# Identity products in eleven more waits, and one weight quarter of the second expert stage loaded early

## What is computed

```python
for layer in range(DEPTH_2):
    u = x * (1.0 + sc1) + sh1
    mix = _mixer(u, ...)
    x = _layernorm(DEEPNORM_ALPHA * x + (1.0 + g1) * mix, ...)
    u = x * (1.0 + sc2) + sh2
    ff = _dense_swiglu(u, ...) if layer % 2 == 0 else _moe_swiglu(u, ...)
    x = _layernorm(DEEPNORM_ALPHA * x + (1.0 + g2) * ff, ...)
```

## Time and profile before

| | us |
|---|---|
| median of 3 runs | 2059.11 |
| lowest and highest | 2055.4 and 2060.55 |
| profiled execution, its own time | 2051.38 |
| its span, first to last instruction | 2049.6 |
| TensorE busy in the span | 1951.5 (95%) |
| VectorE busy | 649.2 (32%) |
| ScalarE busy | 170.3 (8%) |
| mean granted clock of TensorE | 0.986 |

### The profile page before, as it was taken

How to read it: one execution, slowest core, us unless ns; L and a number is a source line. 1 busy time by engine, 2 the same in 40 slices (tenths; PEclk the granted TensorE clock), 3 DMA queues, 4 the chain that set the end, 5 groups by cost and what they waited for, 6 DMA issues and landing times.

```text
span 2049.6 us, 68398 instructions
## 1 busy us (share of the span) xinstructions
PE 1951.5 (95%) x31337; PEld 1567.6 (76%) x31337; DVE 649.2 (32%) x1411; ACT 170.3 (8%) x369; POOL 17.3 (1%) x66
## 2 busy tenths in 40 slices
PE   6999999999999989999999999998999999999996
PEld 4787468777777857648776577588999989989895
DVE  5586333222222232164332523530011110111104
ACT  2002010000000002000000110010000000000000
POOL 1000000000000000000000000000000000000000
PEclk9999999999999999999999999999999999999998
DMA  9998559999999995327766733279999999999992
GB/s 350 314 389 330 214 215 397 420 422 423 421 421 425 420 398 213 142 77 276 261 213 233 267 109 123 103 289 392 411 389 413 405 406 415 403 413 406 405 364 114
DMA packets 179139, 656.00 MB, mean 320 GB/s; under 512 B 16212, under 2 KB 20724, under 8 KB 170868
## 3 DMA queue, kind: packets, MB, share of 16 engines
q1 hardware_dynamic: 170528, 647.41, 80.5%
q0 software_dynamic: 1456, 5.24, 0.7%
q10 hardware_dynamic: 7076, 2.20, 0.5%
HBM read 653.76 MB, written 1.05 MB: 319 GB/s over the span
## 4 chain that ended last, share of the span: by engine, by line
PE 90%; DVE 5%; DMA 3%; issue 2%; SPq 0%; DVEq 0%; ACT 0%
PE ps L1844 88%; DMA ring<-in_moe_w_gate_dram 2%; PE ps L1852 1%; DMA ring<-in_w_ada_dram 1%; DVE stat L1103 0%; DVE arena L1508 0%; DVE arena L1303 0%; DVE hT L991 0%; DVE x L1212 0%; DVE tok L978 0%; DVE tok L1211 0%; DVE newton L971 0%; DVE hT L1086 0%; DVE x L1097 0%; DVE arena L1177 0%
## 5 line engine op out<-in xcount | busy, mean ns | idle before, releaser
L1844 PE MATMUL ps<-arena,ring 128*64 128x80 f32 (+2 forms) x25216 | 877.5, 230 | 23.2 <-issue 18.1
L1844 PEld LDWEIGHTS ps<-arena,ring 128*64 128x64 f32 (+1 forms) x25216 | 859.8, 138 | 50.3 <-issue 40.4
L1844 PE MATMUL ps<-hT,ring 128*128 128x256 f32 (+1 forms) x1680 | 359.4, 385 | 4.2 <-DVE stat L995 2.2
L1844 PEld LDWEIGHTS ps<-hT,ring 128*128 128x128 f32 (+1 forms) x1680 | 308.2, 189 | 51.0 <-issue 2.5
L1844 PE MATMUL ps<-ring,arena 128*64 128x512 f32 (+1 forms) x880 | 273.8, 595 | 1.5 <-DVE stat L1774 1.1
L1844 PE MATMUL ps<-arena 128*128 128x128 f32 (+6 forms) x1576 | 209.1, 307 | 14.0 <-DVE arena L1711 5.6
L1844 PEld LDWEIGHTS ps<-ring,arena 128*64 128x64 f32 (+1 forms) x880 | 104.5, 159 | 150.8 <-issue 147.2
L1844 PEld LDWEIGHTS ps<-arena 128*128 128x128 f32 (+4 forms) x1576 | 138.3, 166 | 67.6 <-issue 31.1
L1469 DVE MEMSET ps<- 128x480 f32 x68 | 28.9, 425 | 278.5 <-ACT arena L742 273.6
L1844 PE MATMUL ps<-ring,hT 128*128 128x512 f32 (+2 forms) x256 | 87.6, 500 | 0.0
L1844 PEld LDWEIGHTS ps<-ring,hT 128*128 128x128 f32 x256 | 46.1, 190 | 38.1 <-issue 36.2
(11 more groups left out here) (325 smaller groups left out, 797.9 us busy)
## 6 DMA issues: line engine op xcount, KB each, us to landing
ring<-in_moe_w_gate_dram SPq DMA_DIRECT2D x128, 704.0 KB, 8.0
ring<-in_moe_w_up_dram SPq DMA_DIRECT2D x128, 704.0 KB, 9.2
ring<-in_moe_w_down_dram SPq DMA_DIRECT2D x176, 512.0 KB, 10.5
ring<-in_w_gate_dram SPq DMA_DIRECT2D x32, 2048.0 KB, 14.8
ring<-in_w_up_dram SPq DMA_DIRECT2D x32, 2048.0 KB, 14.1
ring<-in_w_down_dram SPq DMA_DIRECT2D x32, 2048.0 KB, 12.3
ring<-in_w_in_dram SPq DMA_DIRECT2D x19, 2048.0 KB, 13.9
ring<-in_w_ada_dram SPq DMA_DIRECT2D x12, 2048.0 KB, 15.7
```

The source lines that it names most:

```text
L1844: ins = pe.matmul(*args, **kw)
```

## The change

Three things change. (1) `keep_busy` is called in eight more places of the run and with 5 instead of 3 in the three tile transposes: 21 identity products more. (2) SP loads the second gate quarter of expert 0's first half right behind the first eleven down pieces, after a wait for `x_normed` 7 (VectorE's first normed tile at the end of layer 1's mixer): three pieces go to free columns of another buffer and one to ring columns behind the held pieces. The gate's first quarter of the next half then takes the places where the second quarter was loaded before, at the same waits for `piece_used`. (3) TensorE does the first half of expert 0 in straight code, `first_half_in`, instead of a loop of two passes, because its second gate quarter is read from other places. That is 704 instructions of matmuls and weight loads more. Counts that the gate's semaphores are compared with become one quarter lower (`row_count`).

The diff, without blank context and without its part in `second_all`, which is not run:

```diff
@@ -271,6 +271,7 @@
         gate_row = [sem(f"gate_row{k}") for k in range(KQ)]
         up_row = [sem(f"up_row{k}") for k in range(KQ)]
         down_row = [sem(f"down_row{f}") for f in range(TH)]
+        early_row = [sem(f"early_row{k}") for k in range(KQ)]
         piece_used = sem("piece_used")
         gate_clear, y_clear = sem("gate_clear"), sem("y_clear")
         rows_ready = sem("rows_ready")
@@ -326,6 +327,8 @@
         held_gate = flat[:, GATE_AT:UP_AT].rearrange("p (k n) -> p k n", k=KQ)
         held_up = flat[:, UP_AT:DOWN_AT].rearrange("p (k n) -> p k n", k=KQ)
         held_down = flat[:, DOWN_AT:DOWN_AT + TH * D].rearrange("p (f n) -> p f n", f=TH)
+        EARLY_AT = DOWN_AT + TH * D
+        early_gate = [view(9600 + j * FH, FH) for j in range(KQ - 1)] + [flat[:, EARLY_AT:EARLY_AT + FH]]
         START = None
@@ -468,9 +471,12 @@
             def load_quarter(w, e, v, q, at, place, full, n):
                 for j in range(KQ):
                     if n is None:
                         left_by_ring(at + (j + 1) * FH)
+                    elif isinstance(n, int) and n == 1 and q == 0 and at == GATE_AT:
+                        sp.wait_ge(piece_used, j + 1)
                     else:
                         use = j + (at // QUARTER) * KQ
                         sp.wait_ge(piece_used, used_by(n, use) if q else used_by(n - 1, 2 * KQ + use))
@@ -491,12 +497,17 @@
             load_quarters(0, 0, 0, None)
             load_downs(0, 0, None)
-            for place, full, w, first in ((held_gate, gate_row, wg, 0), (held_up, up_row, wu, KQ)):
-                for j in range(KQ):
-                    sp.wait_ge(piece_used, first + j + 1)
-                    sp.dma_start(place[:, j, :], expert_cols(w, 0, 0, FH)[:, KQ + j, :]).then_inc(full[j], 16)
-            for q in range(2):
-                load_quarters(0, 1, q, 1)
+            sp.wait_ge(H["x_normed"], 7)
+            for j in range(KQ):
+                if j == KQ - 1:
+                    left_by_ring(EARLY_AT + FH)
+                sp.dma_start(early_gate[j], expert_cols(wg, 0, 0, FH)[:, KQ + j, :]).then_inc(early_row[j], 16)
+            load_quarter(wg, 0, 1, 0, GATE_AT, held_gate, gate_row, 1)
+            for j in range(KQ):
+                sp.wait_ge(piece_used, KQ + j + 1)
+                sp.dma_start(held_up[:, j, :], expert_cols(wu, 0, 0, FH)[:, KQ + j, :]).then_inc(up_row[j], 16)
+            load_quarter(wu, 0, 1, 0, UP_AT, held_up, up_row, 1)
+            load_quarters(0, 1, 1, 1)
             with sp.Fori(1, NE2) as e:
                 load_quarters(e, 0, 0, e * 2)
                 load_downs(e - 1, 1, e * 2)
@@ -2040,6 +2051,7 @@
             pe.wait_ge(consts_ready, 1)
             pe.wait_ge(H["tokens_normed"], 1)
             token_transposes(tok)
+            keep_busy(2)
             hT_ready(1)
             s = take()
@@ -2166,8 +2178,10 @@
             ada_turn(1, 6, bank, 0)
             ada_product(1, 8)
             ada_turn(1, 7, bank, 4).then_inc(v_full, 1)
+            keep_busy(3)
             pe.wait_ge(H["tokens_normed"], 2)
             token_transposes(tok)
+            keep_busy(1)
             hT_ready(2)
             pe.wait_ge(got_router, 80)
@@ (in the TensorE program)
+            def row_count(full, n, kk):
+                if full is up_row or isinstance(n, int) and n == 0:
+                    return n * 32 + 16 * (kk + 1)
+                return n * 32 + 16 * kk
@@ -2382,15 +2408,21 @@
             def second_slots(q, cap):
-                def quarter(w, full, n, kk, bank):
+                gate_rows = [held_gate[:, k, :] for k in range(KQ)]
+                up_rows = [held_up[:, k, :] for k in range(KQ)]
+                def quarter(w, full, n, kk, bank, early=False):
                     for k in range(KQ):
                         pe.wait_ge(rows_ready, n * (2 * KQ) + (kk * KQ + (k + 1)))
-                        pe.wait_ge(full[k], n * 32 + (kk * 16 + 16))
+                        if early:
+                            pe.wait_ge(early_row[k], 16)
+                        else:
+                            pe.wait_ge(full[k], row_count(full, n, kk))
                         for f in range(TH):
                             at = f % BANK_TILES * cap
                             for c in range(2):
                                 last = mm(ps[c * HALF:(c + 1) * HALF, bank + f // BANK_TILES, at:at + cap],
-                                          w[:, k, f * P + c * HALF:f * P + (c + 1) * HALF], x_rows[:, k, :],
+                                          w[k][:, f * P + c * HALF:f * P + (c + 1) * HALF], x_rows[:, k, :],
                                           start=False, stop=(k == KQ - 1), skip_group_check=True)
                         last.then_inc(piece_used, 1)
                     return last
@@ -2398,9 +2430,17 @@
                 def half_in(n):
                     with pe.Fori(0, 2) as kk:
                         pe.wait_ge(gate_clear, n + 1)
-                        quarter(held_gate, gate_row, n, kk, GATE_BANK)
+                        quarter(gate_rows, gate_row, n, kk, GATE_BANK)
                         pe.wait_ge(q["up_full"], n + 1)
-                        quarter(held_up, up_row, n, kk, UP_BANK)
+                        quarter(up_rows, up_row, n, kk, UP_BANK)
+                def first_half_in():
+                    pe.wait_ge(gate_clear, 1)
+                    quarter(gate_rows, gate_row, 0, 0, GATE_BANK)
+                    pe.wait_ge(q["up_full"], 1)
+                    quarter(up_rows, up_row, 0, 0, UP_BANK)
+                    quarter(early_gate, gate_row, 0, 1, GATE_BANK, True)
+                    quarter(up_rows, up_row, 0, 1, UP_BANK)
                 def half_down(n, y_cleared):
@@ -2454,7 +2494,7 @@
                     last.then_inc(q["side_full"], 1)
                 dispatch_to(START, 1)
-                half_in(0)
+                first_half_in()
                 half_in(1)
                 half_down(1, 1)
                 dispatch_to(0, 3)
@@ -2496,7 +2536,7 @@
                 with pe.Else():
                     second_all(PH[2])
-            FILL = (3, 3)
+            FILL = (5, 5)
             def find_slots(layer, ne):
@@ -2534,6 +2574,8 @@
                     for c in range(9, ADA_CHUNKS):
                         last = ada_turn(1, c, bank, 4 * (c - 8))
                     last.then_inc(v_full, 1)
+                if layer:
+                    keep_busy(1)
                 hT_ready(3 + 2 * layer)
                 pe.wait_ge(got_layer, 64 * (layer + 1))
                 feature_major(glow_w, h_rhs, (0,), gv_(), cols=lambda f: 0, m=16).then_inc(v_full, 1)
```

More of the change, by code:

```diff
@@ L2243, in first_all @@
                 pe.wait_ge(q["y_free"], NE1)
+            def row_count(full, n, kk):
+                if full is up_row or isinstance(n, int) and n == 0:
+                    return n * 32 + 16 * (kk + 1)
+                return n * 32 + 16 * kk
             def second_all(q):
                 def part_in(n, kk):
-                    for which, (w, full) in enumerate(((held_gate, gate_row), (held_up, up_row))):
-                        for k in range(KQ):
-                            pe.wait_ge(full[k], n * 32 + 16 * (kk + 1))
+                    for which, full in enumerate((gate_row, up_row)):
+                        rows = [(held_up if which else held_gate)[:, k, :] for k in range(KQ)]
+                        if which == 0 and isinstance(n, int) and n == 0 and kk == 1:
+                            rows = early_gate
+                            for k in range(KQ):
+                                pe.wait_ge(early_row[k], 16)
+                        else:
+                            for k in range(KQ):
+                                pe.wait_ge(full[k], row_count(full, n, kk))
                         for j, (lo, hi) in enumerate(dense_spans):
@@ L2256, in part_in @@
                                 for k in range(KQ):
-                                    last = mm(ps[:, 4 + which, (f - lo) * T:(f - lo + 1) * T], w[:, k, f * P:(f + 1) * P],
+                                    last = mm(ps[:, 4 + which, (f - lo) * T:(f - lo + 1) * T], rows[k][:, f * P:(f + 1) * P],
                                               hT[:, kk * KQ + k, :], start=(k == 0), stop=(k == KQ - 1))
```

## The result

On one chip, six runs each: 2040.96 us (2038.03 to 2044.62) after, 2057.26 us before; ratio 0.9922 [0.9905, 0.9939], so 16 us faster. The forecast was 2049.7, 9.4 less than before, with 2043 to 2060 as its range: the right way, and too little. Two executions in the whole record, of 2898 and 5132 us, stand far outside all others and are left out of the medians. The profiled execution of the changed kernel has a span of 2040.1 us, that of before 2049.6: 9.5 us between the two, almost the sum itself. So the question is where the other 7 us come from, and whether the 9.5 is made up as the sum says.

A forecast was written before the change was run, and what follows sets the result against it. TensorE was taken as the bound, slowed where its clock falls behind waits. Products -11.7, their cost 0, early load 0 and written-out code +2.3 gave -9.4 us, from a median of 2059.1 to 2049.7 us; range 2043 to 2060.

The forecast's parts named there:

- the sum: Whole kernel: products' gain -11.7, their cost 0, early load 0, written-out code +2.3, together -9.4 us.
- TensorE and its clock as the bound: Whole run: TensorE is 90% of the last-ending chain, and work takes twice as long where its clock falls to 0.50.
- The products' cost, 0: At TensorE's waits: the 21 identity products, 0.90 us each, all fit; overruns taken as 0, ends 0 to 0.5 us.
- Nothing in the sum depends on where an execution lies among them.: Whole kernel: the -9.4 us from a profiled execution 7.7 us under the median applies unchanged to the median, 2059.1 us.
- the sum had 11.7: Up to the second expert stage: products filling waits prevent clock falls, saving half the TensorE time at 0.50, 11.7 us.
- the decay gates, 1.7: Decay gates: products save 1.7 us in layer 1 and 0 in layer 0, whose clock was already at 1.00.
- The written-out code, +2.3: Expert 0's first half: its written-out second pass becomes a first pass with code-loading gaps, costing 2.3 us, ends 0.5 and 3.8.
- The early load, 0: Second expert stage's start: loading expert 0's second gate quarter early gains TensorE 0 us, ends -0.6 and 0.
- A, free code: Expert 0's first half: written-out code costs nothing, being fetched ahead; 2047.4 us, chance 0.10.
- B, waits for weights: Second expert stage's start: gaps are waits for weights and the load's 6.9 us lead lasts; 2040.5 us, chance 0.07.
- C, falls that stay behind transposes: Products hold the clock only in block 1's first projections and layer 1's decay gates; -1.1 us, 2058.0, chance 0.20.
- D: Second stage's expert loop: 704 more instructions ahead make its code reload in later rounds; 38 us more, 2088 us, chance 0.06.

The follow-up runs named there:

- products_padded: products_only with 30 identity products added in the branch of the first expert stage that isn't run; 2047.64 us, ratio 0.994.
- loop_kept: products_padded measured once more, beside the changed kernel on one chip; 2045.07 us, ratio 0.9941 against the kernel before.
- late_load: The changed kernel with SP issuing the second gate quarter behind TensorE's first four pieces, in the order of before; 2043.03 us, ratio 0.9927.
- five_more: The changed kernel with five more identity products ahead of layer 0's transposes and 59 in the branch that isn't run; 2046.98 us, ratio 0.9944.
- before_padded: The kernel before with 21 identity products in the branch that isn't run, moving the loop's code by 84 instructions; 2079.45 us, ratio 1.0096.
- b_again: The kernel before, measured again without any edit; 2055.34 us, ratio 0.9992.
- before_moved: The kernel before with 51 identity products in the branch that isn't run, moving the loop's code by 204 instructions; 2058.24 us, ratio 1.0006.
- load_and_code_only: The changed kernel without the 21 identity products, keeping the early load and the written-out first half; 2061.11 us, ratio 1.001.
- 17 and 18: loop_kept and the changed kernel run on one chip; 2045.07 us (0.9941) and 2040.76 us (0.9918), with the second expert stage timed by itself across profiles.
- products_only: The kernel before with the 21 identity products alone, loads and loop as before; 2073.06 us, ratio 1.0079.

## Why the prediction was wrong

**TensorE and its clock as the bound: right.** In the changed kernel's profile all stretches at 0.50 that the working counted are gone, and both routers run in 2.0 to 2.1 us. The products don't hold the clock everywhere, though. Of the eleven profiles that have all 21 of them, none falls at the first six places (the first projections, the first router, the decay gates of both layers, layer 0's mixer end and layer 1's start), but four (products_padded, loop_kept, late_load, five_more) fall behind layer 1's router, among or just behind the 16 transposes there, for 3.41 to 10.24 us.

**The products' cost, 0: right.** Two of the tightest waits keep 0.21 and 0.24 us.

**Which step failed.** "Nothing in the sum depends on where an execution lies among them." It does. The profiled execution of before, 7.7 us under the median, was one with few and short falls; an ordinary one has more for the products to save. One instruction shows it: the first of the five identity products behind layer 1's router, which all kernels have. It starts at these times in profiles that run none of the 21 products: before (1336.57 in the earlier trace rows), before_padded (1338.63), and b_again, before_moved and load_and_code_only:

```profile
1340.77 4.54 PE L1844 MATMUL ps<-ident 128*128 128x512 f32 x10
```

```profile
1341.84 6.14 PE L1844 MATMUL ps<-ident 128*128 128x512 f32 x10
```

```profile
1345.41 6.17 PE L1855 MATMUL ps<-ident 128*128 128x512 f32 x10
```

And in the changed kernel's first and fourth profile:

```profile
1327.81 4.54 PE L1855 MATMUL ps<-ident 128*128 128x512 f32 x10
```

```profile
1325.72 4.54 PE L1855 MATMUL ps<-ident 128*128 128x512 f32 x10
```

(1326.67 and 1330.35 in the two between.) The means are 1340.6 and 1327.6: up to here the change is worth 13.0 us, and 13.7 at the start of the next 64 products, since some of the profiles run these five at the low level. The first profiles of before and after show 8.8, and the sum had 11.7. Of the 2.9 that this pair lacks, 1.6 are a fall that the changed kernel's profile has at 162 us and the one of before has not (32 products take 5.47 us there, not 3.84): an execution's falls again. For one term the cause was tried by itself: the decay gates, 1.7 in the sum because layer 0's was "already at 1.00: 0", are worth 3.4.

**The written-out code, +2.3: right where it stands, wrong as a sum.** It cost 2.8 us up to the end of the second half's quarters, and 3.5 came back behind. The working compared first with second passes of the same code and took all that follows as fixed; but all code behind it lies elsewhere too, and its gaps changed from 10.0 to 6.5 us. That the gaps are fewer is shown; why this place is better is not. Over ten profiles the term, with the early load, measures -0.2 and not +2.3 (17 and 18). With the 13.7 that makes 13.9 us, where the sum had 9.4; the four comparisons on medians show 12.1 to 17.5, so how much of the first one's 16.3 is scatter stays open.

**The early load, 0: right.** late_load is as fast.

**The rivals.** A, free code: over the whole stage the code costs about nothing, as A had it, but by another cause, since its gaps are there. B, waits for weights: the time, 2040.96, lies beside B's 2040.5, and that is luck. late_load is as fast without the lead, and the stage itself is no shorter. C, falls that stay behind transposes: refuted at the first router, at layer 0's mixer end and at layer 1's start, which ran at 1.00 in all eleven profiles; behind layer 1's router a fall still comes in some executions. The rule on transposes that stood beside it ("TensorE: Matmul & The Clock Gate", "Part 4: PE-mode transpose", in the Trainium skill) would have kept the falls at those three places too; the trace disagrees, with 1.00 in the stretches from 926.86 and 1171.91 us. D had 0.06 and did not come in this kernel, but its mechanism is real and large: 84 instructions decide over some 20 us. The text looked for it in the 704 instructions; the 21 products' 84 would have brought it, and the 704 take it away again. That the forecast's products were worth their gain at all hung on this. The sum did not see it, and that it came out well is luck.

## What to carry to other kernels

Where a clock falls behind waits, one profile is one draw: set the profiled execution's clock beside that of the other runs, cost the terms on an ordinary execution, and count a wait that happened not to be followed by a fall in the one profile as one that often is. Where two profiles differ, time each stage by itself before giving the difference to a change in one of them. Before believing that a few added instructions cost only their time, count how a long loop behind them lies in the code, and look for transfers of code in its later rounds; dead code in a branch that isn't run is a cheap way to try it. A wait that is filled with work must really be a wait at that point of the program: behind a jump it may be one for code.

## What the runs showed that was not expected

- A loop whose code stays loaded in every round of one kernel is loaded anew in some rounds of another, with 84 instructions more ahead of it: in products_only nine transfers and 7.2 us standing each time, and a clock at 1.2 GHz behind it. Not every round does it: in their profiles 2 of the rounds of products_only and before_padded, more of after_padded.
- One program falls at different waits in different executions, and spreads over 2051 to 2068 us with it, at mean clocks from 0.987 down to 0.978. With the waits filled the spread is 2038 to 2045.
- Behind a taken jump over a branch that isn't run TensorE stood for 7.13 us, in what the profile of before shows as a wait for VectorE alone. The Trainium skill ("Runtime: NRT & Kernel Launch", "Instruction fetch mechanics") says that a taken branch outside what is loaded forces a fetch; the trace agrees, with that number as an upper bound, since the first 0.8 us of it are still VectorE's.
